# Moving five DMA additions per channel-mixer stage onto VectorE, with a new order of its first pipelined chunk and of some table loads

## The chip, the cores and the metric

One core of one Trainium2 chip runs the whole program in one launch. The metric is the device time of one execution in microseconds. The kernel before takes 1023.12 us in the median of three runs (1019.76 to 1023.62).

## The reference

The function is a decoder trunk of two layers over 256 tokens of width 1024, all in float32. Each layer has three post-norm sublayers:

```
x = LN(a*x + 0.5*swiglu(x, ffn1_w_in, ffn1_w_out))
x = LN(a*x + mixer(x))            # layer 0: differential attention + causal pooling; layer 1: HGRN2
x = LN(a*x + 0.5*swiglu(x, ffn2_w_in, ffn2_w_out))

def swiglu(x, w_in, w_out):       # w_in: 1024 x 5632, w_out: 2816 x 1024
    gate, up = split(x @ w_in, 2)
    return (silu(gate) * up) @ w_out
```

So there are six stages: F0, AB, F1, F2, C, F3. The four F stages are the SwiGLU channel mixers, and the change touches only them.

## The kernel before

**Precision.** Each float32 weight and activation is split into a high part rounded to the matmul type and a low part, the rest. ScalarE makes the high part (`split_hi`, L494 to L500, from `raw` into `w_hi`), VectorE subtracts to get the low part (`split_lo`, L967 to L973, into `w_lo`), and TensorE multiplies high by high, high by low and low by high.

**Weights.** They come in units of 1 MB (128 x 2048 float32) into `raw`, which has three buffers. SyncE issues the loads in order, each in two DMAs, and unit n may start when unit n-3 has been used: for an ordinary unit when its `split_lo` is done (L371 to L380).

**An F stage.** The hidden width 2816 is cut into 11 chunks of 256. Chunks 0, 1 and 10 go the ordinary way. Chunks 2 to 9 (`FIRST_FM` is 2) are pipelined; each takes three units: two of `w_in` (n+1 and n+2 in the code of ScalarE and VectorE, for the *next* chunk) and one of `w_out` (n). In chunks 0 to 9 the down projection of a pair of 128-blocks is not done with eight block products but with seven, of sums of blocks (a Strassen-like scheme): `weight_sums` (L981) and `hidden_sums` (L1011) form the sums on VectorE, `split_sums_hi`/`split_sums_lo` and `hid_early_hi`/`hid_late_hi` and their `_lo` partners split them.

**TensorE in a pipelined chunk** (`feature_chunk`, L2011): `up_block` 0, late products of the chunk before, `up_block` 1, products, `up_block` 2, products, `up_block` 3, products. All four `up_block`s use the one PSUM bank `G[0]`, so each waits (L1978) until ScalarE's `up_copy` (L564 to L570) has copied the block before it out. In a trace `up_block` is the lines L1981 and L1988, a product is L1995.

**Order on ScalarE in a pipelined chunk** (L620 to L636): `split_hi(n+1)`, `hid_early_hi`, `up_copy` 0, `split_hi(n+2)`, `hid_late_hi`, `up_copy` 1, `split_sums_hi`, `up_copy` 2, `split_plain_hi`, `up_copy` 3, `gates_silu`. **On VectorE** (L1176 to L1194): `up_add`, `up_product` and `hidden_sums` of the chunk before, the two parts of `weight_sums`, `hid_early_lo`, `split_lo(n+1)`, `hid_late_lo`, `beside` (table work in some chunks), `split_lo(n+2)`, `split_sums_lo`, `split_plain_lo`.

**GpSimd** adds the two halves of each gate by a DMA with accumulation (`add_gates`, L1694), two per pipelined chunk. In F0 it also loads tables between them: `poolw` (256 KB), `band` (768 KB) and then `ln_gb` (two of 512 KB) follow directly on the gate additions of chunk 3 (L1733 to L1737).

**End of an F stage.** The seven products are combined into the residual `x_tok`. ScalarE copies two of them out (`copied_out`), VectorE forms `kept[1]` and `kept_both` (`sums_out`, L1228, `moved_out`), and GpSimd then adds them to `x_tok` by five accumulating DMAs (`add_sums`, L1703), in an order that its semaphores set. VectorE's `norm_stats` (L1087) waits for these DMAs before it adds the last PSUM sums to `x_tok` and takes the statistics. VectorE's order there (L1196 to L1215) is `sums_out`, `split_lo(n)`, `ffn_hidden`(token tile 0), `split_lo(n+1)`, `last_hidT(0)`, `split_lo(n+2)`, `norm_stats(0)`, half of `norm_gain(0)`, `ffn_hidden`(tile 1), the other half, `last_hidT(1)`, `norm_scale(0)`, `split_lo(n+3)`. TensorE needs `ffn_hidden`(tile 1), line L1137, to transpose the last hidden tile (L1965), and goes on to the next stage behind it.

Of the kernel before, what the change touches and what calls it, by code (L numbers as in the profile page):

```python
# [25 lines left out]
P = 128  # L26
# [49 lines left out]
def build(nc, x, positions, ln_gain, ln_bias, ffn1_w_in, ffn1_w_out, ffn2_w_in, ffn2_w_out, ab_w_in, ab_w_o,  # L76
          diff_lambda, diff_subln, pool_w, pool_scale, c_w_in, c_w_o, c_norm, hgrn_gamma, consts, out):
    with ExitStack() as ctx:
# [3 lines left out]
        def sem(name):  # L82
            return ctx.enter_context(nc.semaphore(name))
# [63 lines left out]
        gate_added = [sem(f"gate_added{j}") for j in range(2)]  # L147
        up_added, x_added = sem("up_added"), [sem(f"x_added{i}") for i in range(5)]
        gate_silu, hid_product = sem("gate_silu"), sem("hid_product")
# [325 lines left out]
        def _(act):  # L475
# [18 lines left out]
            def split_hi(n):  # L494

                if n >= N_UNITS:
                    return
                landed(n)
                freed(free_by[n])
                nc.scalar.copy(w_hi[:, slot_of[n]], raw[:, n % RAW]).then_inc(hi_ready, 1)  # L500
# [77 lines left out]
            def ffn(name, m):  # L578
# [17 lines left out]
                else:  # L596
# [18 lines left out]
                    ffn_silu(name, 1, 1, G[1])  # L615
                split_hi(s0 + 6)
                hidT_copy(name, 1, G[0])
                split_plain_hi(s0 + 7)
                last = NC - 2
                for c in range(FIRST_FM, NC - 1):  # L620
                    n = s0 + 3 * c + 1
                    split_hi(n + 1)
                    hid_early_hi(name, c - 1)
                    up_copy(name, c, 0)
                    split_hi(n + 2)
                    hid_late_hi(name, c - 1)
                    up_copy(name, c, 1)
                    split_sums_hi(name, n)
                    up_copy(name, c, 2)
                    if c == last:  # L630
                        act.wait_ge(plain_used, N_PROD * (f + 1))
                        nc.scalar.activation(kept[0], PROD[0], ACT.Copy, scale=NORMS[name][1]).then_inc(copied_out, 1)
                        split_hi(n + 3)
                    else:
                        split_plain_hi(n + 3)
                    up_copy(name, c, 3)  # L636
                    gates_silu(name, c)
# [320 lines left out]
        def _(dve):  # L958
# [128 lines left out]
            def norm_stats(name, t):  # L1087
                n, factor = NORMS[name]
                y = Y if name in FFN else Y_MIX[name]
                if name in FFN:  # L1090
                    for i in ((2, 4), (0, 1, 3))[t]:
                        dve.wait_ge(x_added[i], 16 * (SILUS[name] + 1))
                for h in range(2):
# [45 lines left out]
            def ffn(name, m):  # L1139
# [38 lines left out]
                for c in range(FIRST_FM, NC - 1):  # L1178
# [10 lines left out]
                    beside(name, c)  # L1189
                    split_lo(n + 2)  # L1190
                    split_sums_lo(name, n)
                    if c < last:
# [11 lines left out]
                ffn_hidden(name, 0, G[0], 4, ffn_tok[:, 1, 0])  # L1204
                split_lo(n + 1)
                last_hidT(name, 0)
                split_lo(n + 2)
                norm_stats(name, 0)
                norm_gain(name, 0, (0,))
# [6 lines left out]
            def beside(name, c):  # L1216
# [8 lines left out]
                if name == BEFORE_C and c in (7, 8, 9):  # L1225
                    lower_bound(c - 7)

            def sums_out(name):  # L1228
# [442 lines left out]
        def _(pool):  # L1671
# [27 lines left out]

            def add_to_x(i, t, cs, part):  # L1700
                pool.dma_start(x_tok[:, t, cs], part, accum_op=ALU.add).then_inc(x_added[i], 16)

            def add_sums(name):  # L1703
                f = SILUS[name]
                low, high = slice(0, 512), slice(512, D)
                pool.wait_ge(copied_out, 2 * f + 1)
                add_to_x(0, 1, high, kept[0])
                pool.wait_ge(copied_out, 2 * f + 2)
                add_to_x(1, 1, low, SUM_PLACES[name][:, 0])
                add_to_x(2, 0, low, SUM_PLACES[name][:, 0])  # L1710
                pool.wait_ge(moved_out, 2 * f + 1)
                pool.wait_ge(x_added[1], 16 * (f + 1))
                add_to_x(3, 1, low, kept[1])
                pool.wait_ge(moved_out, 2 * f + 2)
                pool.wait_ge(x_added[2], 16 * (f + 1))
                pool.dma_start(x_tok[:, 0].rearrange("p (h f) -> p h f", h=2),
                               kept_both.unsqueeze(1).to_broadcast([P, 2, 512]), accum_op=ALU.add
                               ).then_inc(x_added[4], 16)

            pool.wait_ge(lo_ready, RAW + 1)  # L1720
            with nc.allow_non_contiguous_dma(reason="a few columns of parameters"):
# [10 lines left out]
                               ).then_inc(S["pool_tables_landed"], 16)  # L1732
                add_gates("F0", (2, 3))  # L1733
                pool.dma_start(poolw, pool_w[0].rearrange("g p f -> p g f")).then_inc(S["pool_tables_landed"], 16)
                pool.dma_start(band, consts[:, C_BAND:C_DECAY].rearrange("p (g f) -> p g f", g=4)
                               ).then_inc(S["pool_tables_landed"], 16)
            load_gb(0)  # L1737
            for n, name in enumerate(ORDER):
# [18 lines left out]
                if name in FFN:  # L1757
                    add_gates(name, range(4 if name == "F0" else FIRST_FM, NC - 1))
                    add_sums(name)
                norm(n)  # L1760
# [723 lines left out]
```

## Time and profile before

| | |
|---|---|
| median of three runs | 1023.12 us |
| time of the profiled execution | 1022.99 us |
| span of the profile | 1020.4 us |
| TensorE matmul busy | 969.8 us, 95% |
| VectorE busy | 861.3 us, 84% |
| ScalarE busy | 619.4 us, 61% |
| GpSimd busy | 111.1 us, 11% |
| mean granted TensorE clock | 0.975 of full |
| DMA traffic | 199.38 MB, mean 195 GB/s |

The span runs from the first to the last instruction. Granted clock 1.00 is 2.4 GHz and 0.50 is 1.2 GHz. A busy share counts a matmul at the low clock as fully busy, so TensorE's 95% holds slow time too. In timeline rows the bracket gives the idle time of that engine before the row and what ended it.

### The profile page before, as it was taken

What the parts mean: (1) busy time and instruction counts of PE and PEld (TensorE: products, weight loads), DVE (VectorE), ACT (ScalarE), POOL (GpSimd) and SP (SyncE); (2) the same over time, 40 slices, a digit from 0 to 9 for tenths busy, and PEclk for the clock granted to TensorE, in tenths of its full rate; (3) what the DMA queues carried; (4) which work ended last, traced back from release to release, by engine and by line L of the source; (5) the groups of instructions that cost most, each with busy time, mean ns of one, the idle gap of its engine ahead of it and who ended that gap; (6) DMA issues with size and microseconds to landing.
All of it is one profiled execution on the core that took longest, in us unless ns stands there. A gap on an engine that the chain in (4) does not pass through costs nothing.

```text
span 1020.4 us, 13819 instructions
## 1 busy us (share of the span) xinstructions
PE 969.8 (95%) x4904; PEld 818.9 (80%) x4904; DVE 861.3 (84%) x1188; ACT 619.4 (61%) x727; POOL 111.1 (11%) x148
## 2 busy tenths in 40 slices
PE   9798999899998999997989999989999998999995
PEld 7687888688886888885878888868888886888884
DVE  5878998696797899985879999879998997898885
ACT  6566667255745667672656667646898645667660
POOL 0111011100210011011001010200100200011020
PEclk9899999899998999998989999999999998999998
DMA  8767768644557676885476676936432756676862
GB/s 293 242 211 229 240 199 235 195 166 143 191 202 250 188 205 199 246 226 159 163 217 191 211 209 198 282 118 196 133 125 83 241 175 204 184 204 200 245 160 58
DMA packets 141935, 199.38 MB, mean 195 GB/s; under 512 B 7312, under 2 KB 114336, under 8 KB 141744
## 3 DMA queue, kind: packets, MB, share of 16 engines
q1 hardware_dynamic: 126032, 173.56, 52.0%
q0 software_dynamic: 15280, 24.46, 11.6%
q8 instruction: 39, 0.64, 0.3%
q10 hardware_dynamic: 560, 0.52, 0.2%
q14 instruction: 24, 0.20, 0.1%
HBM read 182.78 MB, written 1.05 MB: 180 GB/s over the span
## 4 chain that ended last, share of the span: by engine, by line
PE 72%; DVE 13%; DMA 9%; issue 3%; ACT 2%; POOL 0%; SPq 0%; DVEq 0%; ACTq 0%; POOLq 0%
PE psum L1981 19%; PE psum L1995 12%; PE psum L1988 10%; PE psum L1790 9%; PE psum L1794 9%; PE psum L1799 9%; DMA x_tok<-arena 5%; DVE w_lo L972 4%; DMA raw<-in_ffn_w_in 4%; PE psum L2371 1%; PE psum L1783 1%; DVE w_lo L1008 1%; PE psum L2357 1%; DVE stats L1098 1%; DVE arena L1410 1%
## 5 line engine op out<-in xcount | busy, mean ns | idle before, releaser
L972 DVE TENSOR_TENSOR w_lo<-raw,w_hi 128x2048 fp32r<-128x2048 f32 x125 | 285.1, 2285 | 14.8 <-ACT w_hi L500 14.4
L1981 PE MATMUL psum<-xT,w_hi 128*128 128x512 f32 x1024 | 261.0, 398 | 19.7 <-ACT ffn_tok L570 18.9
L500 ACT CAST w_hi<-raw 128x2048 fp32r<-128x2048 f32 x125 | 237.9, 1911 | 44.8 <-DMA raw<-in_ffn_w_in 32.4
L1981 PEld LDWEIGHTS psum<-xT,w_hi 128*128 128x128 f32 x1024 | 195.7, 192 | 65.8 <-ACT ffn_tok L570 22.8
L1988 PEld LDWEIGHTS psum<-xT,w_lo 128*128 128x128 f32 x1024 | 143.1, 195 | 11.1 <-DVE w_lo L972 0.7
L1988 PE MATMUL psum<-xT,w_lo 128*128 128x256 f32 x1024 | 146.1, 286 | 0.5 <-DVE w_lo L972 0.5
L1790 PE MATMUL psum<-w_hi,xT 128*128 128x512 f32 x447 | 128.6, 398 | 0.5 <-DVE arena L1519 0.4
L1799 PE MATMUL psum<-w_hi,xT 128*128 128x512 f32 x447 | 124.7, 390 | 0.2 <-DVE xT L1076 0.2
L1794 PE MATMUL psum<-w_lo,xT 128*128 128x512 f32 x447 | 124.7, 390 | 0.0
L1698 POOL DMA_DIRECT2D ffn_tok<-ffn_tok x64 | 54.4, 850 | 520.8 <-ACT ffn_tok L570 520.8
L1799 PEld LDWEIGHTS psum<-w_hi,xT 128*128 128x128 f32 x447 | 83.9, 188 | 18.3 <-DVE xT L1076 0.5
L1794 PEld LDWEIGHTS psum<-w_lo,xT 128*128 128x128 f32 x447 | 83.9, 188 | 17.7
L1790 PEld LDWEIGHTS psum<-w_hi,xT 128*128 128x128 f32 x447 | 80.8, 188 | 16.2 <-issue 0.8
L570 ACT COPY arena<-psum 128x512 f32<-128x512 f32 x64 | 37.6, 587 | 92.2 <-PE psum L1988 92.2
L1008 DVE TENSOR_TENSOR w_lo<-arena,w_hi 128x2048 fp32r<-128x2048 f32 x35 | 80.0, 2284 | 10.6 <-ACT w_hi L512 10.6
L978 DVE TENSOR_TENSOR w_lo<-raw,w_hi 128x1536 fp32r<-128x1536 f32 x36 | 63.2, 1755 | 19.3 <-ACT w_hi L506 19.1
L1995 PE MATMUL psum<-w_hi,hT_hi 128*128 128x512 f32 x232 | 76.2, 399 | 0.0
L1995 PE MATMUL psum<-w_lo,hT_hi 128*128 128x512 f32 x232 | 75.4, 395 | 0.3
L512 ACT CAST w_hi<-arena 128x2048 fp32r<-128x2048 f32 x36 | 69.0, 1916 | 3.4 <-DVE arena L996 3.4
L1995 PE MATMUL psum<-w_hi,hT_lo 128*128 128x512 f32 x232 | 69.8, 393 | 0.0
L570 ACT COPY ffn_tok<-psum 128x512 f32<-128x512 f32 x64 | 37.5, 586 | 49.1 <-PE psum L1988 49.1
L506 ACT CAST w_hi<-raw 128x1536 fp32r<-128x1536 f32 x36 | 53.4, 1484 | 11.7 <-PE psum L1995 10.7
(219 smaller groups left out, 1189.5 us busy)
## 6 DMA issues: line engine op xcount, KB each, us to landing
raw<-in_ffn_w_in SPq DMA_DIRECT2D x170, 512.0 KB, 5.4
raw<-in_ffn_w_out SPq DMA_DIRECT2D x88, 512.0 KB, 4.4
raw<-in_c_w_in SPq DMA_DIRECT2D x32, 512.0 KB, 4.7
ffn_tok<-ffn_tok POOLq DMA_DIRECT2D x64, 128.0 KB, 4.5
raw<-in_ab_w_in SPq DMA_DIRECT2D x16, 512.0 KB, 5.4
x_tok<-arena POOLq DMA_DIRECT2D x16, 256.0 KB, 6.3
raw<-in_ab_w_o SPq DMA_DIRECT2D x8, 512.0 KB, 4.4
raw<-in_c_w_o SPq DMA_DIRECT2D x8, 512.0 KB, 4.0
```

Of the source, the lines that this page charges most:

```text
L500: nc.scalar.copy(w_hi[:, slot_of[n]], raw[:, n % RAW]).then_inc(hi_ready, 1)
L512: nc.scalar.copy(w_hi[:, SUMS], SUM_PLACES[name].rearrange("p a f -> p (a f)")).then_inc(sums_hi, 1)
L570: nc.scalar.copy((UPS[name] if b // 2 else GATES)[:, b % 2], G[0]).then_inc(up_copied, 1)
L972: nc.vector.tensor_tensor(w_lo[:, slot_of[n]], raw[:, n % RAW], w_hi[:, slot_of[n]].bitcast(F32), ALU.subtract).then_inc(lo_ready, 1)
L978: nc.vector.tensor_tensor(w_lo[:, PLAIN, 0:1536], raw[:, n % RAW, 512:], w_hi[:, PLAIN, 0:1536].bitcast(F32), ALU.subtract).then_inc(plain ...
L1008: nc.vector.tensor_tensor(w_lo[:, SUMS], SUM_PLACES[name].rearrange("p a f -> p (a f)"), w_hi[:, SUMS].bitcast(F32), ALU.subtract).then_in ...
L1790: nc.tensor.matmul(dst, a_hi, b_hi, start=first, stop=False)
L1794: ins = nc.tensor.matmul(dst, a_hi, b_lo, start=False, stop=final and last)
L1799: ins = nc.tensor.matmul(dst, a_lo, b_hi, start=False, stop=final and last)
L1981: nc.tensor.matmul(G[0], w_hi[:, slot_of[n + kh], at:at + P], xT_both[:, 4 * kh + k].rearrange("p a s -> p (a s)"), start=kh == k == 0, st ...
L1988: ins = nc.tensor.matmul(G[0][:, 0:SEQ], w_lo[:, slot_of[n + kh], at:at + P], xT_hi[:, 4 * kh + k], start=False, stop=kh == 1 and k == 3)
L1995: return nc.tensor.matmul(PROD[p], a[:, A_OF[p] * P:(A_OF[p] + 1) * P], w[:, slot, part * 512:(part + 1) * 512], start=start, stop=stop)
```

## The change

It has four parts. In every F stage the five accumulating DMAs into `x_tok` go, with their semaphores and with the waits in `norm_stats`, and four VectorE additions of 512 columns and one of 1024 take their place: two before `last_hidT(0)` (the 1024-column one adds `kept_both` to both halves of tile 0) and three before `norm_stats(0)`. In the first pipelined chunk (c = 2) of every F stage ScalarE and VectorE take a new order. In F0 alone ScalarE copies the second hidden transposes (`hidT_copy`) before `split_hi(s0+6)`. In F0 GpSimd's table loads are spread: `poolw` behind the gate additions of chunk 4, `band` behind those of chunk 5, `ln_gb` behind those of chunk 6.

```diff
@@ ScalarE, ffn
-                split_hi(s0 + 6)
-                hidT_copy(name, 1, G[0])
+                if m == 0:
+                    hidT_copy(name, 1, G[0])
+                    split_hi(s0 + 6)
+                else:
+                    split_hi(s0 + 6)
+                    hidT_copy(name, 1, G[0])
...
+                    if c == FIRST_FM:
+                        up_copy(name, c, 0)
+                        hid_early_hi(name, c - 1)
+                        split_hi(n + 1)
+                        hid_late_hi(name, c - 1)
+                        up_copy(name, c, 1)
+                        split_sums_hi(name, n)
+                        up_copy(name, c, 2)
+                        split_hi(n + 2)
+                    else:
+                        split_hi(n + 1)
+                        hid_early_hi(name, c - 1)
+                        up_copy(name, c, 0)
+                        split_hi(n + 2)
+                        hid_late_hi(name, c - 1)
+                        up_copy(name, c, 1)
+                        split_sums_hi(name, n)
+                        up_copy(name, c, 2)
@@ VectorE, norm_stats
-                if name in FFN:
-                    for i in ((2, 4), (0, 1, 3))[t]:
-                        dve.wait_ge(x_added[i], 16 * (SILUS[name] + 1))
@@ VectorE, ffn
-                    split_lo(n + 2)
-                    split_sums_lo(name, n)
+                    if c == FIRST_FM:
+                        split_sums_lo(name, n)
+                        split_lo(n + 2)
+                    else:
+                        split_lo(n + 2)
+                        split_sums_lo(name, n)
...
                 split_lo(n + 1)
+                dve.wait_ge(moved_out, 2 * f + 2)
+                add_to_x(0, slice(0, 512), SUM_PLACES[name][:, 0])
+                x0 = x_tok[:, 0].rearrange("p (h f) -> p h f", h=2)
+                step(nc.vector.tensor_tensor(x0, x0, kept_both.unsqueeze(1).to_broadcast([P, 2, 512]), ALU.add))
                 last_hidT(name, 0)
                 split_lo(n + 2)
+                add_to_x(1, slice(512, D), kept[0])
+                add_to_x(1, slice(0, 512), SUM_PLACES[name][:, 0])
+                add_to_x(1, slice(0, 512), kept[1])
                 norm_stats(name, 0)
...
+            def add_to_x(t, cs, part):
+
+                step(nc.vector.tensor_tensor(x_tok[:, t, cs], x_tok[:, t, cs], part, ALU.add))
@@ GpSimd
-            def add_to_x(i, t, cs, part):
-                pool.dma_start(x_tok[:, t, cs], part, accum_op=ALU.add).then_inc(x_added[i], 16)
-
-            def add_sums(name):
...
-                add_gates("F0", (2, 3))
+                add_gates("F0", (2, 3, 4))
                 pool.dma_start(poolw, pool_w[0].rearrange("g p f -> p g f")).then_inc(S["pool_tables_landed"], 16)
+                add_gates("F0", (5,))
                 pool.dma_start(band, consts[:, C_BAND:C_DECAY].rearrange("p (g f) -> p g f", g=4)
                                ).then_inc(S["pool_tables_landed"], 16)
+            add_gates("F0", (6,))
             load_gb(0)
...
-                    add_gates(name, range(4 if name == "F0" else FIRST_FM, NC - 1))
-                    add_sums(name)
+                    add_gates(name, range(7 if name == "F0" else FIRST_FM, NC - 1))
```

## Rows read from the trace of the kernel before

**Rows 1.** Page: the chain's shares, three costly groups, the weight loads' landing time.
```profile
PE 72%; DVE 13%; DMA 9%; issue 3%; ACT 2%; POOL 0%; SPq 0%; DVEq 0%; ACTq 0%; POOLq 0%
...
L972 DVE TENSOR_TENSOR w_lo<-raw,w_hi 128x2048 fp32r<-128x2048 f32 x125 | 285.1, 2285 | 14.8 <-ACT w_hi L500 14.4
...
L500 ACT CAST w_hi<-raw 128x2048 fp32r<-128x2048 f32 x125 | 237.9, 1911 | 44.8 <-DMA raw<-in_ffn_w_in 32.4
...
L978 DVE TENSOR_TENSOR w_lo<-raw,w_hi 128x1536 fp32r<-128x1536 f32 x36 | 63.2, 1755 | 19.3 <-ACT w_hi L506 19.1
...
raw<-in_ffn_w_in SPq DMA_DIRECT2D x170, 512.0 KB, 5.4
```

**Rows 2.** Waits of the whole run: waiter, releaser, us in total, times, longest.
```profile
DVE x_tok L1096 <- DMA x_tok<-arena: 18.9, 3, 8.1
...
PE psum L1981 <- ACT ffn_tok L570: 18.9, 5, 4.2
...
PE psum L1965 <- DVE ffn_tok L1137: 17.4, 3, 7.6
```

**Rows 3.** Timeline of PE, F0 and F1: start us, duration us, instruction.
```profile
39.55 0.62 PE L1995 MATMUL psum<-w_hi,hT_lo 128*128 128x512 f32 x2
...
59.02 1.98 PE L1981 MATMUL psum<-xT,w_hi 128*128 128x512 f32 x8
...
74.95 1.98 PE L1981 MATMUL psum<-xT,w_hi 128*128 128x512 f32 x8
...
316.33 1.98 PE L1981 MATMUL psum<-xT,w_hi 128*128 128x512 f32 x8
...
339.00 1.98 PE L1981 MATMUL psum<-xT,w_hi 128*128 128x512 f32 x8
...
343.15 1.98 PE L1981 MATMUL psum<-xT,w_hi 128*128 128x512 f32 x8
```

**Rows 4.** Timeline of ACT in F1, chunks 2 and 3.
```profile
321.47 1.90 ACT L500 CAST w_hi<-raw 128x2048 fp32r<-128x2048 f32 x1 [4.70 <-DMA raw<-in_ffn_w_in]
...
323.90 0.58 ACT L570 COPY ffn_tok<-psum 128x512 f32<-128x512 f32 x1
...
341.97 0.59 ACT L570 COPY ffn_tok<-psum 128x512 f32<-128x512 f32 x1
```

**Rows 5.** Timeline of DVE in F1, chunk 2: first weight sum, then chunk 3's first step.
```profile
320.48 1.22 DVE L990 TENSOR_TENSOR arena<-raw 128x1024 f32<-128x1024 f32 x1
...
338.66 0.69 DVE L1044 TENSOR_TENSOR arena<-arena 128x512 f32<-128x512 f32 x1 [0.29 <-ACT arena L570]
```

**Rows 6.** Windows: stretch, PE, PEld, DVE, ACT, POOL busy, granted clock, DMA share, GB/s.
```profile
83.20:86.00 2.80, 0.00 (x0) 0.00 (x0) 0.49 (x2) 2.73 (x4) 0.00 (x0) 1.00 0.91 303
324.50:331.10 6.60, 6.57 (x21) 5.59 (x22) 5.18 (x4) 3.26 (x4) 1.04 (x2) 0.57 0.91 274
198.20:203.80 5.60, 5.60 (x15) 4.32 (x16) 4.53 (x5) 0.38 (x1) 0.00 (x0) 0.50 0.00 0
477.60:481.90 4.30, 4.27 (x14) 3.47 (x15) 3.70 (x5) 0.37 (x1) 0.00 (x0) 0.68 0.00 0
671.90:676.30 4.40, 4.36 (x14) 3.56 (x15) 3.81 (x5) 0.37 (x1) 0.00 (x0) 0.66 0.01 4
533.50:550.20 16.70, 16.70 (x90) 14.42 (x89) 16.36 (x18) 11.54 (x13) 1.68 (x2) 1.00 0.65 184
```

**Rows 7.** Chain of F0's chunk 3: start us, us, what.
```profile
70.34 12.91 DMA raw<-in_ffn_w_in
```

**Rows 8.** Timeline of DVE at the end of F1.
```profile
462.24 0.42 DVE L1242 TENSOR_TENSOR hT_lo<-psum,hT_hi 128x256 fp32r<-128x256 f32 x1 [1.67 <-ACT hT_hi L653]
...
473.00 0.69 DVE L1096 SCALAR_TENSOR_TENSOR x_tok<-psum,x_tok 128x512 f32<-128x512 f32 x1 [8.14 <-DMA x_tok<-arena]
```

**Rows 9.** Timeline of PE at the end of F3, which had no such wait.
```profile
1005.50 0.38 PE L1965 MATMUL psum<-ident,ffn_tok 128*128 128x128 f32 x2
...
1008.45 0.62 PE L1790 MATMUL psum<-w_hi,hT_hi 128*128 128x512 f32 x2
```

More of the change, by code:

```diff
@@ L147, in build @@
         gate_added = [sem(f"gate_added{j}") for j in range(2)]
-        up_added, x_added = sem("up_added"), [sem(f"x_added{i}") for i in range(5)]
+        up_added = sem("up_added")
         gate_silu, hid_product = sem("gate_silu"), sem("hid_product")
@@ L621, in ffn @@
                     n = s0 + 3 * c + 1
[L622 to L629, printed above, removed]
+                    if c == FIRST_FM:
[16 more added lines that the diff above has]
+                        up_copy(name, c, 2)
                     if c == last:
@@ L1698, in add_gates @@
                         pool.dma_start(GATES[:, j, 0:SEQ], GATES[:, j, SEQ:], accum_op=ALU.add).then_inc(gate_added[j], 16)
-            def add_to_x(i, t, cs, part):
-                pool.dma_start(x_tok[:, t, cs], part, accum_op=ALU.add).then_inc(x_added[i], 16)
-            def add_sums(name):
[L1704 to L1718, printed above, removed]
             pool.wait_ge(lo_ready, RAW + 1)
```

## The prediction

> **What bounds the kernel now.** I read the chain of waits first. TensorE is 72% of the way to the end, and what is not TensorE is mostly VectorE and DMA [rows 1]. So the question is where TensorE stands still, and the list of waits answers it. Two waits stand out: five times it waits for ScalarE's `up_copy` before an `up_block`, 18.9 us in all, and three times for VectorE's `ffn_hidden` before it transposes the last hidden tile, 17.4 us in all [rows 2]. The timelines put the first kind at chunk 2 of all four F stages and once in chunk 4 of F0, the second at the ends of F0, F1 and F2. The windows add a second loss: behind the long stalls the granted clock is low, 0.57 for 6.6 us in F1's chunk 2, 0.50 (1.2 GHz), 0.68 and 0.66 at the three ends, while behind the 2.80 us stall of F0's chunk 4 it never left 1.00 [rows 6]. VectorE's 84% busy share is no bound there: VectorE is itself waiting in those places.
>
> **Part 1, the additions to x.** In F1 VectorE stands 8.14 us before `norm_stats(0)`, for the accumulating DMAs [rows 8]; over the three stages it is 18.9 us, and three times, so F3 has none of it [rows 2]. The change removes the wait and adds five operations. An addition of 512 columns with both operands in SBUF takes 0.69 us, one of 1024 columns 1.22 us [rows 5], and each waits for its own signal, some 0.04 us. Before `last_hidT(0)` come 0.73 + 1.26 = 2.0 us, where VectorE had 1.67 us idle [rows 8]; 0.3 us sticks out. Before `norm_stats(0)` come 3 x 0.73 = 2.2 us. So each stage pays 2.5 us from its wait and the gain is 18.9 - 3 x 2.5 = 11.4 us. It reaches the end in full, because `ffn_hidden`(tile 1) follows `norm_stats(0)` at a fixed distance and TensorE stands for it: its 17.4 us become 6.0, 2.0 in each stage. In F3 the five operations fall into gaps in front of TensorE's last sums and cost 0; if that cover were gone they would cost 2.2 us. GpSimd loses five DMA issues a stage and nothing is queued behind them but the `rstd` power, which waits for VectorE anyway. What is late next is VectorE's own string from `norm_stats(0)` to `ffn_hidden`.
>
> **Part 2, the clock at these ends.** From the transposes to the next stage's transposes TensorE took 5.6, 4.3 and 4.4 us at clocks 0.50, 0.68 and 0.66 [rows 6]. The same instructions took 1008.45 - 1005.50 = 2.95 us in F3, after no such stall [rows 9]. With a stall of 2.0 us, below the 2.80 us that left the clock at 1.00 [rows 6], I expect 2.4 GHz to be kept: gain 2.65 + 1.35 + 1.45 = 5.4 us. Bounds are 0 and 5.4; I take 5.4, since 2.0 lies under the nearest row. The Trainium skill (TensorE: Matmul & The Clock Gate, Part 4, on transposes) speaks against this: a transpose does not count as engine activity in the way a matmul does, so the two transposes behind the stall would lengthen the quiet stretch. No row here separates that. By it the sum would be 5.4 us smaller, which is the first rival below.
>
> **Part 3, the first pipelined chunk.** A steady chunk takes 74.95 - 59.02 = 15.93 us. F1's chunk 2 takes 339.00 - 316.33 = 22.67, a surplus of 6.7 [rows 3]. Its cause is ScalarE's order: `up_copy` 0 sits behind `split_hi(n+1)`, which stands 4.70 us for its weights, so that the copy starts at 323.90 [rows 4], though the block, begun at 316.33, needs only some 3 us. F2 and F3 repeat the pattern with surpluses of 6.7 and 7.0. In F0 a front part waits for other things: from the end of its late products (39.55 + 0.46) to 59.02 it takes 19.0, where a steady chunk has 15.93 - (343.15 - 339.00) = 11.8, surplus 7.2 [rows 3]. All of it includes the low clock, so all is removable: 27.6 us. In the new order the copy goes first and waits for TensorE alone. The load of n+1 lands at the same moment as before, its cast runs beside `up_block` 1, and `up_copy` 1 is ready some 0.6 us before it is needed.
>
> Something is given back. `split_hi(n+2)` now sits behind `up_copy` 2, which can run only when the third block is done. The second block starts 4.15 after the chunk, the third 11.8 / 3 = 3.9 later, and it runs 3 us: in F1's times 316.33 + 4.15 + 3.9 + 3 = 327.4. Then follow the copy 0.5, the cast 1.9, `split_lo(n+2)` 2.2 and `split_plain_lo` 1.7 [rows 1] (`split_sums_lo`, moved ahead, fills VectorE's wait for that cast and costs nothing; uncovered it would cost another 2.2): VectorE reaches chunk 3's first step at 333.7 instead of 338.66 [rows 5], a gain of 5.0, while TensorE would start chunk 3 at 339.00 - 6.7 = 332.3. VectorE thus is at +1.4 beside TensorE, where it was at -0.3. The chain through `hidden_sums`, `hid_early_hi` and `up_copy` 0 has 343.15 - (341.97 + 0.59) = 0.6 us of slack [rows 3, 4]. So TensorE stands 1.4 + 0.3 - 0.6 = 1.1 us once in chunk 3, too short for the clock, and VectorE catches up in the rest of that chunk. Gain 5.6 in F1 and 5.9 in F0 and F3. In F2 VectorE is the bound behind chunk 2 (16.36 of 16.70 us busy, a chunk in 16.7 instead of 15.93 us) [rows 6], so only its own gain of 4.9 counts. Sum 5.9 + 5.6 + 4.9 + 5.9 = 22.3 us. F0's early `hidT_copy` I cost at nothing: its block then ends its high passes sooner but still waits for `split_lo(s0+6)`, which does not move. If that cover were gone it would give up to 0.7.
>
> **Part 4, the tables.** In F0 the second load of chunk 3 lands after 12.91 us [rows 7], against 5.4 in the median [rows 1]; 2 MB of tables (`poolw`, `band`, `ln_gb`) were issued just ahead. TensorE stands 2.80 us for it [rows 6]. Spread over three chunks the largest piece is 1 MB: at (12.91 - 5.4) / 2 = 3.8 us per MB it delays one load by 3.8, and the load had room for 12.91 - 5.4 - 2.8 = 4.7. Gain 2.8; bounds 0 and 2.8. GpSimd's gate additions that the tables are moved past come first, so nothing of chunk 4 or 5 waits for them, and the tables are read a hundred microseconds later.
>
> **Sum.** 11.4 + 5.4 + 22.3 + 2.8 = 41.9 us off the profiled execution's 1022.99 gives 981.1; this execution stands 0.13 under the median of 1023.12, so 981.
>
> **Rivals.**
> *The clock stays low at the ends of F0, F1 and F2.* For it: TensorE still stands 2.0 us, with transposes behind. Against: 2.80 us did nothing. Part 2 falls away: 986.5. Chance 0.13.
> *Weights late in chunk 3.* In chunk 2 the DMA engines are already 0.91 busy at 274 GB/s [rows 6], and the load that follows `split_lo(n+2)` is issued only as TensorE enters chunk 3, so it lands when ScalarE wants it, without slack. At 3 us late in each of four stages 12 us go back: 993. Against: the load before it has landed by then, and 5.4 us just does. Chance 0.17.
> *The lag does not fade, and the kernel gets slower.* Loads wait for `split_lo` three units back, so a late subtraction makes a late load, a late cast and a late subtraction again. Place: chunks 3 to 9 of each F stage and the last one, 32 chunks in all. If each kept a stall like the 2.8 us of F0's chunk 4, 90 us would be lost against 42 gained: 1071. It decides from 42 / 32 = 1.3 us per chunk. Against: VectorE idles some 1.2 us in a plain chunk, so a lag shrinks. Chance 0.04.
> *The change does not do what it says.* If the additions cannot start where they stand, because TensorE or GpSimd still holds one of their operands, or the copies move without effect, the time stays within 5 us of before: 1020. The DMAs that read the same operands were on their way before VectorE's idle time began, so chance 0.02.
> *VectorE does not lag in chunk 3*, so that the 1.1 us in three stages and F2's share come back too: 977. Chance 0.12.
>
> **How the numbers follow.** My forecast of 981 has 0.52. The range must reach the clock rival and the late weights and the case without the lag: 974 to 997, which leaves out the last cases of slow and no effect and a margin. About 0.5%, or 5 us, is what a measurement of this kernel can tell from no change. Faster by more than that: 0.52 + 0.13 + 0.17 + 0.12 = 0.94. Within it: the change without effect, 0.02. Slower: 0.04.
>
> **What would show it.** In the changed profile VectorE's wait for x DMAs is gone; `norm_stats(0)` of F1 starts about 5.6 us sooner relative to its stage's last products; TensorE's three stalls there are 2.0 us and the windows behind show clock 1.00 and 2.95 us. In chunk 2 TensorE runs through at clock 1.00; in chunk 3 it stands about 1.1 us before `up_block` 1; F2 gains less than the rest. In F0 no load takes over 10 us. I would be wrong on part 3 if chunk 3 or later chunks exceed 15.93 by more than 1.2 us in F1, on part 2 if the clock after a 2 us stall is below 1.00, on part 1 if the additions take more than 0.75 us each.

## The result, and the profile after

The changed kernel takes 982.13 us in the median of four runs (980.97 to 982.53). Its ratio to the kernel before, run beside it, is 0.9603 with a 95% interval of [0.958, 0.9626]. The forecast was 981 in a range of 974 to 997. The profiled execution took 982.20 us with a span of 980.5 us. TensorE's mean granted clock rose from 0.975 to 0.997, and DMA traffic fell from 199.38 to 193.10 MB. One run of the kernel before, beside the second group of experiments below, took 1198.9 us at a granted clock of 0.748 and is left out of the ratios.

The page of the kernel after: busy time of TensorE and VectorE, the chain's shares, and two of the groups that [rows 1] shows of before.

```profile
PE 955.4 (97%) x4904; PEld 805.7 (82%) x4904; DVE 875.5 (89%) x1208; ACT 619.6 (63%) x727; POOL 93.5 (10%) x128
...
PE 77%; DVE 15%; ACT 3%; DMA 2%; issue 2%; SPq 1%; POOL 0%; DVEq 0%; ACTq 0%
...
L986 DVE TENSOR_TENSOR w_lo<-raw,w_hi 128x2048 fp32r<-128x2048 f32 x125 | 285.2, 2285 | 20.3 <-ACT w_hi L500 19.7
...
L500 ACT CAST w_hi<-raw 128x2048 fp32r<-128x2048 f32 x125 | 238.2, 1913 | 26.2 <-DMA raw<-in_ffn_w_in 15.4
```

TensorE's share of the chain went from 72 to 77% and DMA's from 9 to 2%. The two groups take the same time for each instruction as before; only their idle time differs. So nothing became faster in itself: 969.8 us of TensorE busy time became 955.4 because less of it ran at the low clock, and the rest of the gain is idle time that went.

The waits of the whole run, after (waiter, releaser, us in total, times, longest), to lay beside [rows 2]:

```profile
ACT w_hi L500 <- DMA raw<-in_ffn_w_in: 15.4, 16, 2.4
...
PE psum L1972 <- DVE ffn_tok L1148: 5.4, 3, 1.8
...
PE psum L1988 <- ACT ffn_tok L570: 4.4, 6, 1.0
```

VectorE's wait of 18.9 us for the additions to `x_tok` has no row any more. TensorE's wait for `up_copy` went from 18.9 to 4.4 us and that for `ffn_hidden` from 17.4 to 5.4.

TensorE at the ends of F0, F1 and F2 after (start us, duration us, instruction, idle before): the transposes of the last hidden tile, and those of x for the next stage.

```profile
186.63 0.44 PE L1972 MATMUL psum<-ident,ffn_tok 128*128 128x128 f32 x2 [1.80 <-DVE ffn_tok L1148]
...
189.67 1.04 PE L1790 MATMUL psum<-ident,x_tok 128*128 128x128 f32 x8
...
452.50 0.44 PE L1972 MATMUL psum<-ident,ffn_tok 128*128 128x128 f32 x2 [1.82 <-DVE ffn_tok L1148]
...
638.43 0.44 PE L1972 MATMUL psum<-ident,ffn_tok 128*128 128x128 f32 x2 [1.81 <-DVE ffn_tok L1148]
```

The window behind the first of these stalls (PE, PEld, DVE, ACT, POOL busy, granted clock, DMA share, GB/s), beside the 0.50 of [rows 6]:

```profile
186.60:189.60 3.00, 2.97 (x14) 2.49 (x15) 2.66 (x5) 0.37 (x1) 0.00 (x0) 1.00 0.00 0
```

Each stall is 1.8 us, the clock behind it 1.00, and the way to the next transposes 3.04 us where it was 5.6.

VectorE at the end of F0 after, which holds all five additions:

```profile
175.34 0.68 DVE L1252 TENSOR_TENSOR x_tok<-x_tok,arena 128x512 f32<-128x512 f32 x1
176.06 1.22 DVE L1224 TENSOR_TENSOR x_tok<-x_tok,arena 128x1024 f32<-128x1024 f32 x1
...
179.86 2.14 DVE L1252 TENSOR_TENSOR x_tok<-x_tok,arena 128x512 f32<-128x512 f32 x3
182.03 0.69 DVE L1107 SCALAR_TENSOR_TENSOR x_tok<-psum,x_tok 128x512 f32<-128x512 f32 x1
```

The three additions of tile 1 take 182.03 - 179.86 = 2.2 us directly ahead of tile 0's statistics, and 2.2 is more than the 1.8 for which TensorE still stands.

What they replaced can be read more closely than the prediction did. The chain of waits of the kernel before at the end of F1:

```profile
451.62 7.59 DMA x_tok<-arena
...
461.04 11.88 DMA x_tok<-arena
```

The last of the five DMAs (`kept_both` onto tile 0) was issued at 461.04, behind GpSimd's wait of 6.40 us for one of the earlier ones to land, and landed 11.88 us later at 472.92; the statistics started at 473.00 [rows 8]. The other four had landed by 465.40. So it was one DMA, late in its place and long in itself, that held VectorE there. Whether the same five DMAs in another order, tile 0's first, would have removed part of the wait was not tried.

TensorE in chunks 2 and 3 of F1 after (`up_block` 0 and 2 of chunk 2, 0 and 1 of chunk 3, and the start of chunk 4), beside [rows 3]:

```profile
301.94 1.98 PE L1988 MATMUL psum<-xT,w_hi 128*128 128x512 f32 x8
...
310.43 2.11 PE L1988 MATMUL psum<-xT,w_hi 128*128 128x512 f32 x8 [0.25 <-ACT ffn_tok L570]
...
318.42 1.98 PE L1988 MATMUL psum<-xT,w_hi 128*128 128x512 f32 x8
323.70 2.12 PE L1988 MATMUL psum<-xT,w_hi 128*128 128x512 f32 x8 [0.97 <-ACT ffn_tok L570]
...
335.62 1.98 PE L1988 MATMUL psum<-xT,w_hi 128*128 128x512 f32 x8
```

Chunk 2 takes 16.48 us instead of 22.67, chunk 3 17.20 instead of 15.93.

### The profile page after: what moved, and what is told of

Same layout as the page of the kernel before. It is cut to its first block, busy times and chain, and to the rows that moved or that the text cites. A ratio compares the mean times of both kernels' runs of the same rounds, so it can differ in the third digit from the quotient of the medians.

```text
span 980.5 us, 13807 instructions
## 1 busy us (share of the span) xinstructions
PE 955.4 (97%) x4904; PEld 805.7 (82%) x4904; DVE 875.5 (89%) x1208; ACT 619.6 (63%) x727; POOL 93.5 (10%) x128
## 2 busy tenths in 40 slices
DMA packets 138544, 193.10 MB, mean 197 GB/s; under 512 B 6992, under 2 KB 114016, under 8 KB 138352
## 4 chain that ended last, share of the span: by engine, by line
PE 77%; DVE 15%; ACT 3%; DMA 2%; issue 2%; SPq 1%; POOL 0%; DVEq 0%; ACTq 0%
PE psum L1988 19%; PE psum L2002 12%; PE psum L1797 10%; PE psum L1801 10%; PE psum L1806 10%; PE psum L1995 10%; DVE w_lo L986 5%; DMA raw<-in_ffn_w_in 2%; ACT w_hi L500 2%; PE psum L2378 1%; PE psum L1790 1%; DVE w_lo L1022 1%; DVE x_tok L1252 1%; PE psum L2364 1%; DVE arena L1436 1%
## 5 line engine op out<-in xcount | busy, mean ns | idle before, releaser
L1988 PE MATMUL psum<-xT,w_hi 128*128 128x512 f32 x1024 | 254.9, 391 | 4.7 <-ACT ffn_tok L570 4.4
L1988 PEld LDWEIGHTS psum<-xT,w_hi 128*128 128x128 f32 x1024 | 191.1, 188 | 50.8 <-ACT ffn_tok L570 10.1
L1995 PEld LDWEIGHTS psum<-xT,w_lo 128*128 128x128 f32 x1024 | 139.7, 190 | 11.6 <-DVE w_lo L986 1.6
L1995 PE MATMUL psum<-xT,w_lo 128*128 128x256 f32 x1024 | 143.0, 282 | 1.4 <-DVE w_lo L986 1.4
```

Source lines behind the costliest of these rows:

```text
L1988: nc.tensor.matmul(G[0], w_hi[:, slot_of[n + kh], at:at + P], xT_both[:, 4 * kh + k].rearrange("p a s -> p (a s)"), start=kh == k == 0, st ...
L1995: ins = nc.tensor.matmul(G[0][:, 0:SEQ], w_lo[:, slot_of[n + kh], at:at + P], xT_hi[:, 4 * kh + k], start=False, stop=kh == 1 and k == 3)
```

## The experiments

Twelve kernels ran, in three groups of four, each group beside runs of the kernel before. The medians of before beside them were 1021.86, 1021.82 (without the run of 1198.9 us) and 1021.52 us, against 1023.37 beside the kernel after; ratios are therefore safer than differences between groups of less than some 2 us.

**The additions alone.** Into the kernel before go only the five VectorE additions, and its accumulating DMAs and waits go out.

```diff
+                dve.wait_ge(moved_out, 2 * f + 2)
+                add_to_x(0, slice(0, 512), SUM_PLACES[name][:, 0])
...
                 norm_stats(name, 0)
...
-                    add_sums(name)
```

> The kernel before with the five additions of each F stage on VectorE and nothing else of the change. My theory (parts 1 and 2): TensorE's three stalls at the ends of F0, F1, F2 (5.05, 7.64, 4.67 us) shrink to about 2 us each (-11.4) and the granted clock behind them stays at 1.00 (-5.4): 1023 - 16.8 = 1006 us. Rival, the clock falls even behind a 2 us stall: 1012. Rival, the additions only pay beside the new chunk order: over 1015.

Measured: 1004.02 us (1001.27 to 1007.71), ratio 0.9826 [0.9791, 0.9862], 17.8 us off where 16.8 were expected. Two windows of this run, behind the stalls of 1.81 and 1.82 us at the ends of F0 and F1 (columns as in the window above):

```profile
194.70:197.70 3.00, 2.97 (x14) 2.49 (x15) 2.65 (x5) 0.37 (x1) 0.00 (x0) 1.00 0.00 0
465.50:468.50 3.00, 3.00 (x11) 2.48 (x12) 2.65 (x5) 0.37 (x1) 0.00 (x0) 0.74 0.01 3
```

The size is confirmed within the interval, which reaches from 14 to 21 us, and the additions need no help from the new order. In the profiled execution (1004.07 us, 18.9 off) 15.8 us of the gain lie at the three ends; 2.7 more lie in chunks 2 and 3, where the stalls are about as long as before and the low clock behind them was shorter. But the same stall in front of the same instructions left the clock at 1.00 in F0 and F2 and lowered it in F1. My bound ("2.0 lies under the nearest row") is thereby no bound.

**The order alone.** The kernel before with the new chunk 2 on both engines:

```diff
+                    if c == FIRST_FM:
+                        up_copy(name, c, 0)
+                        hid_early_hi(name, c - 1)
+                        split_hi(n + 1)
...
+                        split_sums_lo(name, n)
+                        split_lo(n + 2)
```

> The kernel before with the new order of chunk 2 on ScalarE and VectorE and nothing else. My theory (part 3): 5.6 + 5.9 + 4.9 + 5.9 = 22.3 us off, 1001 us; read off the trace of the kernel after, some 20 us, 1003. A 1 us stall before the second block of chunk 3 in each F stage, and the 2.8 us stall of F0's chunk 4 still there or larger, as its tables are not moved. Rival, late weights when only the order is changed: over 1008.

Measured: 1003.95 us (1000.45 to 1010.31), ratio 0.9816 [0.9783, 0.9849], 17.9 us off. Each chunk 3 has the expected stall (0.93 to 0.98 us). What is missing to 22.3 us lies at least in part in F0's chunk 4. Its load in the chain of waits, and TensorE behind it:

```profile
62.84 13.88 DMA raw<-in_ffn_w_in
```

```profile
79.81 3.78 PE L1995 MATMUL psum<-xT,w_hi 128*128 128x512 f32 x8 [6.01 <-ACT ffn_tok L570]
```

```profile
79.80:86.40 6.60, 6.59 (x21) 5.60 (x22) 6.11 (x9) 3.13 (x4) 1.05 (x2) 0.55 0.58 159
```

The stall of 2.80 us [rows 6] is now 6.01, with the clock at 0.55 for 6.6 us behind it: 3.2 us of stall and 3.0 of clock, which the order loses in this execution, with the tables together. Parts 3 and 4 are not additive. This profiled execution, at 1010.31 us, is the slowest of the six: in it chunks 2 and 3 give 21.2 us, chunk 4 takes 5.9 and the three ends, where the DMAs still add to `x_tok`, take 3.1 more than in the profile of before. How much chunk 4 takes in the other five is not shown.

**The tables alone.**

```diff
-                add_gates("F0", (2, 3))
+                add_gates("F0", (2, 3, 4))
                 pool.dma_start(poolw, ...)
+                add_gates("F0", (5,))
                 pool.dma_start(band, ...)
...
+            add_gates("F0", (6,))
```

> The kernel before with the table loads of F0 spread over chunks 4 to 6 and nothing else. My theory (part 4): the 2.8 us stall in F0's chunk 4 goes and nothing comes in its place: 1020.3 us, ratio 0.997. Rival, the load is late for another reason, as unit loads queue behind each other: no change, 1023.

Measured: 1018.63 us in 12 runs (1015.93 to 1020.41), ratio 0.9958 [0.9935, 0.9981]: 3.2 us off, and no stall of TensorE in F0's chunk 4.

**The tables together again, in the kernel after.**

```diff
-                add_gates("F0", (2, 3, 4))
+                add_gates("F0", (2, 3))
                 pool.dma_start(poolw, ...)
-                add_gates("F0", (5,))
...
-            add_gates("F0", (6,))
```

> The kernel after with the F0 table loads in their old places, all 2 MB behind the gate additions of chunk 3. By my part 4 as predicted the 2.8 us stall of chunk 4 comes back and nothing more: 985. What the run with the order alone showed speaks against it: there the same stall had grown to 6.0 us with a slow block behind it. Theory now: with the new order the next loads are wanted sooner, nothing covers more of the tables' time, and the price is that stall of 6 us and some 1.7 us of clock: 982.1 + 7.7 = 990.

Measured: 987.88 us (987.06 to 989.97), ratio 0.9657 [0.9627, 0.9688], 5.8 us more than after. The load in the chain, ScalarE's cast that waits for it, and TensorE:

```profile
62.77 12.39 DMA raw<-in_ffn_w_in
```

```profile
75.19 1.90 ACT L500 CAST w_hi<-raw 128x2048 fp32r<-128x2048 f32 x1 [5.61 <-DMA raw<-in_ffn_w_in]
```

```profile
78.25 3.52 PE L1986 MATMUL psum<-xT,w_hi 128*128 128x512 f32 x8 [4.52 <-ACT ffn_tok L570]
```

The stall is 4.5 us, between the two expectations, and it costs clock as well (this execution, at 989.97 us, is the slowest of the four). The same edit is worth 3.2 us in the kernel before and 5.8 in this one; the intervals of the two overlap, so it is the rows that tell them apart. It is not the same load that is late. ScalarE's two casts of chunk 4 in the kernel before:

```profile
75.01 1.90 ACT L500 CAST w_hi<-raw 128x2048 fp32r<-128x2048 f32 x1
...
83.27 1.90 ACT L500 CAST w_hi<-raw 128x2048 fp32r<-128x2048 f32 x1 [4.77 <-DMA raw<-in_ffn_w_in]
```

There the first `w_in` unit (its halves issued at 67.25 and 67.83, the second landing after 6.01 us) came in time, and the second unit, issued at 69.78 and 70.34 behind all four tables (67.56 to 69.38), was the late one; its cast stands behind `up_copy` 0 and stops TensorE before the third block. With the new order and the tables together it is the first unit, whose second half is issued at 62.77 between the first table (62.02) and the other three (62.79 to 63.85) and takes 12.39 us. Its cast stands ahead of `up_copy` 0, so TensorE stops one block sooner and for longer; the second cast then waits for nothing. Why this half takes 12.39 us where the same half took 6.01 is not settled by these rows.

**Tile 1's additions as DMAs, tile 0's on VectorE.**

```diff
                 split_lo(n + 2)
-                add_to_x(1, slice(512, D), kept[0])
-                add_to_x(1, slice(0, 512), SUM_PLACES[name][:, 0])
-                add_to_x(1, slice(0, 512), kept[1])
                 norm_stats(name, 0)
...
+                if name in FFN and t == 1:
+                    for i in range(3):
+                        dve.wait_ge(x_added[i], 16 * (SILUS[name] + 1))
...
```

In the part left out GpSimd issues three accumulating DMAs again, each on its own semaphore.

> The kernel after, but the three additions to token tile 1 are accumulating DMAs again, issued by GpSimd as before and waited for only ahead of the statistics of tile 1; the two additions to tile 0 stay on VectorE. My theory: the remaining 1.8 us stall at each end is VectorE's string, of which 2.2 us are these three additions, and the DMAs have some 17 us until tile 1's statistics; statistics of tile 0 start when its last sums are done, and TensorE gains 1.8 us in each of F0, F1, F2: 982.1 - 5.4 = 976.7 us, unless VectorE then holds up the next stage's tile 1, which leaves at least 1 us a stage: 979. Rival, the DMAs are late for tile 1 or their traffic delays a weight load: no gain or a loss, 982 or more.

Measured: 975.31 us (974.88 to 975.72), ratio 0.954 [0.9511, 0.9569], below the expectation of 976.7 and clear of the interval of the kernel after. VectorE and TensorE at the end of F0:

```profile
179.55 0.68 DVE L1110 SCALAR_TENSOR_TENSOR x_tok<-psum,x_tok 128x512 f32<-128x512 f32 x1
...
183.71 0.42 DVE L1151 TENSOR_TENSOR ffn_tok<-psum,ffn_tok 128x256 f32<-128x256 f32 x1
```

```profile
184.39 0.38 PE L1984 MATMUL psum<-ident,ffn_tok 128*128 128x128 f32 x2
```

The statistics start where the three additions had stood, the hidden product is ready at 184.1, and TensorE transposes without a stall. VectorE has no wait for an x DMA in this run. So the remaining 1.8 us of the kernel after were its own additions, and three DMAs are fast enough for tile 1's statistics.

**up_copy 0 first in chunk 3 as well**, on top of that kernel.

```diff
                     else:
                         split_hi(n + 1)
-                        hid_early_hi(name, c - 1)
-                        up_copy(name, c, 0)
+                        if c == FIRST_FM + 1:
+                            up_copy(name, c, 0)
+                            hid_early_hi(name, c - 1)
+                        else:
+                            hid_early_hi(name, c - 1)
+                            up_copy(name, c, 0)
```

> The kernel with tile 1's additions as DMAs (975.3 us) and, in chunk 3 of each F stage alone, up_copy 0 ahead of hid_early_hi on ScalarE. Theory of part 3's give-back: the stall before the second block of chunk 3 comes because up_copy 0 stands behind hid_early_hi, which waits for VectorE's late hidden_sums; with the copy first the stalls (0.6 to 1.0 us in each of four stages) go: 975.3 - 3.2 = 972 us. Rival, VectorE's lag then stops TensorE one step later, at the products that need the hidden split: no gain.

Measured: 972.14 us (970.92 to 973.97), ratio 0.9512 [0.9481, 0.9543], the fastest kernel of the study and the 3.2 us below the run before it that were expected. The two ratios' intervals overlap, but the ranges (970.92 to 973.97, 974.88 to 975.72) do not, and in the rows the four stalls are gone. The chain's shares on its page, and TensorE's one remaining stall of over 0.5 us in any chunk 3, in F2:

```profile
PE 87%; DVE 8%; ACT 1%; issue 1%; DMA 1%; POOL 0%; DVEq 0%; SPq 0%; ACTq 0%
```

```profile
510.90 0.73 PE L2018 MATMUL psum<-w_lo,hT_hi 128*128 128x512 f32 x2 [0.89 <-DVE w_lo L1026]
```

The give-back of part 3 was the place of `up_copy` 0 behind a step that needs `hidden_sums`. VectorE starts chunk 3 of F1 1.41 us behind TensorE, as late as in the kernel after; the copy simply does not need it. Only in F2, where VectorE has table work too, does its lateness reach TensorE elsewhere.

**VectorE's order in chunk 2 undone.**

```diff
-                    if c == FIRST_FM:
-                        split_sums_lo(name, n)
-                        split_lo(n + 2)
-                    else:
-                        split_lo(n + 2)
-                        split_sums_lo(name, n)
+                    split_lo(n + 2)
+                    split_sums_lo(name, n)
```

> The kernel after with VectorE's split_lo(n+2) ahead of split_sums_lo again in chunk 2, ScalarE's order unchanged. By part 3 of the prediction the swap fills VectorE's wait for the cast, and without it split_sums_lo is 2.2 us on the way to chunk 3's first step and to TensorE's products of the sums: 982.1 + up to 4 x 2.2 = 986 to 991 us. Rival, the slack takes it: 982.

Measured: 994.24 us (991.91 to 996.52), ratio 0.9735 [0.969, 0.9781], 12.1 us more than after. VectorE and TensorE in F1's chunk 2:

```profile
319.05 2.29 DVE L986 TENSOR_TENSOR w_lo<-raw,w_hi 128x2048 fp32r<-128x2048 f32 x1 [3.41 <-ACT w_hi L500]
321.26 2.28 DVE L1022 TENSOR_TENSOR w_lo<-arena,w_hi 128x2048 fp32r<-128x2048 f32 x1
```

```profile
323.60 0.72 PE L1998 MATMUL psum<-w_lo,hT_hi 128*128 128x512 f32 x2 [2.86 <-DVE w_lo L1022]
```

TensorE stands 2.86 us in all four stages, and then no more in chunk 3; behind two of the four stalls the clock fell. I had bounded the swap by its 2.2 us. It is worth more, some 3 us a stage: ScalarE's new order makes VectorE stand 3.41 us for the cast, and without the swap the low part of the sums, which TensorE wants in this very chunk, stands behind that wait.

**F0's hidT_copy undone.**

```diff
-                if m == 0:
-                    hidT_copy(name, 1, G[0])
-                    split_hi(s0 + 6)
...
+                split_hi(s0 + 6)
+                hidT_copy(name, 1, G[0])
```

> The kernel after with F0's second hidT_copy behind split_hi(s0+6) again. Prediction: nothing, 982.1; the wait for the copy (0.72 us) comes back and the wait for the low part of s0+6 shrinks by as much (1.37 to 0.5). Rival, the early copy delays the split by its own length and costs 0.2 us: 981.9. Both are within what a run can tell, so the rows decide: the start of chunk 2 relative to the split's end.

Measured: 981.69 us (980.69 to 983.71), ratio 0.9612 [0.9569, 0.9654]: nothing, as forecast. The start of F0's chunk 2 in this run, and the same wait in the kernel after:

```profile
34.66 2.11 PE L1984 MATMUL psum<-xT,w_hi 128*128 128x512 f32 x8 [0.73 <-ACT arena L547]
...
37.71 0.74 PE L1991 MATMUL psum<-xT,w_lo 128*128 128x256 f32 x4 [0.47 <-DVE w_lo L982]
```

```profile
38.28 0.74 PE L1995 MATMUL psum<-xT,w_lo 128*128 128x256 f32 x4 [1.37 <-DVE w_lo L986]
```

0.73 + 0.47 = 1.20 us in two waits became 1.37 in one. The cover named in the prediction, `split_lo(s0+6)`, is what holds.

**Longer stalls at the ends.** Three kernels add one, two and five additions on dead scratch to the kernel after, in F0 to F2:

```diff
+                if name != "F3":
+                    for _ in range(2):
+                        step(nc.vector.tensor_tensor(kept[1], kept[1], kept[0], ALU.add))
                 norm_stats(name, 0)
```

With two:

> The kernel after with two further additions of 512 columns (on dead scratch) ahead of the statistics of tile 0 in F0, F1 and F2, 1.45 us each stage, to lengthen TensorE's stall at each end from 1.8 to 3.3 us, with the transposes behind it as before. Theory: the clock stays at 1.00 (in F0's chunk 4 it did behind 2.8 us), and the time rises by 3 x 1.45 = 4.4 us to 986.5. Rival, with transposes behind a stall the clock falls sooner: 1.3 to 2.7 us more for each end, 991 to 994.

With five:

> As the run with two further additions, but with five, 3.6 us each stage: stalls of 5.4 us, as long as before the change. Theory: the low clock comes back too, as it was behind 4.7 to 7.6 us: 982.1 + 3 x 3.6 + 3 x 1.8 = 998 us, and the windows behind the stalls show 0.5 to 0.7. Rival, the low clock before was not of the stall but of what else ran there (the DMAs): 993, clock 1.00.

With one:

> The kernel after with one further addition ahead of the statistics of tile 0 in F0, F1 and F2: stalls of 2.5 us with transposes behind, between 1.8 us (the clock stayed at 1.00 in three of three in the kernel after, and fell in one of three with the additions alone) and 3.25 us (it fell in three of three). If the clock stays: 982.1 + 2.2 = 984.3 us. If it falls each time: 989. I expect it to fall in some and not in others, with a scatter between the runs: 986.

Measured: two 992.09 us (990.44 to 993.76), ratio 0.9698 [0.9663, 0.9732]; five 998.84 (997.82 to 1000.06), ratio 0.9771 [0.974, 0.9802]; one 987.26 (986.89 to 988.46), ratio 0.9662 [0.962, 0.9703]. TensorE's stalls at F0 and F2 with one addition:

```profile
187.91 0.44 PE L1975 MATMUL psum<-ident,ffn_tok 128*128 128x128 f32 x2 [2.52 <-DVE ffn_tok L1148]
...
643.90 0.44 PE L1975 MATMUL psum<-ident,ffn_tok 128*128 128x128 f32 x2 [2.55 <-DVE ffn_tok L1148]
```

From there to the next transposes of x (192.40, 646.93) it is 4.49 us in F0 and 3.03 in F2: the clock fell in the first, and in F1, and stayed in F2; 982.1 + 2.2 + 2 x 1.5 = 987.3. With two additions it fell in all three, and with five too (0.59 for 4.7 us in F0). A window behind the stall at F0's end, with two additions:

```profile
188.00:192.50 4.50, 4.48 (x14) 3.68 (x15) 3.90 (x5) 0.37 (x1) 0.00 (x0) 0.63 0.00 0
```

The sums close: two additions 982.1 + 4.4 of stall + (4.58 + 4.61 + 5.60 - 3 x 3.04) of clock = 992.2; five 982.1 + 10.9 + (4.80 + 4.40 + 4.77 - 3 x 3.04) = 997.8. So my theory for 3.3 us was wrong and its rival's time came (whether because of the transposes, as the rival has it, these runs cannot tell), and the theory for 5.4 us was right. A fall costs 1.4 to 2.6 us here and no more behind 5.4 us than behind 3.3.

**Stalls in the middle of a stage**, with no transposes behind, on the kernel with tile 1's additions as DMAs:

```diff
+                for _ in range({("F0", 5): 4, ..., ("F3", 8): 6}.get((name, c), 0) if b == 0 else 0):
+                    step(nc.scalar.copy(GATES[:, 0], G[0]))
                 nc.scalar.copy((UPS[name] if b // 2 else GATES)[:, b % 2], G[0]).then_inc(up_copied, 1)
```

> The kernel with tile 1's additions as DMAs (975.3 us), with up_copy 0 repeated on ScalarE 4 to 8 times in chunks 5 and 8 of the F stages, so that TensorE stands in the middle of a stage, with matmuls and no transposes behind: 4 times (about 1.9 us of stall) in F0's chunk 5 and F2's chunk 8, 5 (2.6) in F1's 5 and F0's 8, 6 (3.2) in F2's 5, F1's 8 and F3's 8, 8 (4.5) in F3's 5. Theory: the clock depends on how long TensorE stood and not on the transposes: it stays at 1.00 behind 1.9 and falls behind 3.2 and more, as at the ends (three of three at 3.25). Rival, transposes count as rest: without them the clock stays at 1.00 behind 3.2 us too. Stalls alone give 975.3 + 22 = 997 us; each fall adds 1.5 to 2, so 1003 by the theory, 998 to 1000 by the rival.

Measured: 1003.96 us (1002.86 to 1005.83), ratio 0.9825 [0.9781, 0.9869]. Five of the eight stalls (timeline of TensorE):

```profile
91.73 3.44 PE L2002 MATMUL psum<-xT,w_hi 128*128 128x512 f32 x8 [1.86 <-ACT ffn_tok L572]
...
144.15 2.11 PE L2002 MATMUL psum<-xT,w_hi 128*128 128x512 f32 x8 [2.38 <-ACT ffn_tok L572]
...
413.36 3.50 PE L2002 MATMUL psum<-xT,w_hi 128*128 128x512 f32 x8 [3.00 <-ACT ffn_tok L572]
...
604.69 2.12 PE L2002 MATMUL psum<-xT,w_hi 128*128 128x512 f32 x8 [1.76 <-ACT ffn_tok L572]
...
940.33 2.12 PE L2002 MATMUL psum<-xT,w_hi 128*128 128x512 f32 x8 [3.00 <-ACT ffn_tok L572]
```

Windows behind three of them (PE busy, granted clock, DMA share, GB/s):

```profile
91.70:97.70 6.00, 5.97 (x23) 0.72 1.01 306
...
413.30:419.30 6.00, 5.95 (x24) 0.74 0.99 309
...
940.30:946.30 6.00, 5.97 (x30) 1.00 1.01 300
```

The first group's duration tells the clock at a glance: 3.4 to 3.5 us at the low one, 2.1 at the full. It fell behind 1.86 us and not behind 1.76 or 2.38 (twice); of two stalls of 3.00 us in the same place of the chunk it fell behind one; it fell behind 3.75 and 4.24. The theory's order by length holds only at the long end, and the rival as put (no fall behind 3 us) falls too. The time that the theory gave, 1003, came out all the same: the eight stalls add up to 22.4 us, which leaves 6.3 for the four falls.

## Why the prediction was right

The time and the case were right: 982.1 against 981, and none of the rivals came. By its terms, from the two profiled executions (1022.99 to 982.20 us, 40.8 off):

| term | forecast, us | in the traces | by a run of its own |
|---|---|---|---|
| 1 and 2, additions and clock at three ends | 16.8 | 17.1 | 17.8 |
| 3, order of chunk 2 | 22.3 | 20.2 | 17.9 alone |
| 4, tables | 2.8 | 3.0 | 3.2 alone, 5.8 in the kernel after |
| elsewhere | 0 | 0.5 | |

Of the 40.8 us, 0.9 lie outside the profile's span, which became shorter by 39.9.

**Part 1** stands as worked out. The stall at each end is 1.80 to 1.82 us where 2.0 were forecast: a stage pays 2.3 us and not 2.5 for its additions. 17.4 - 5.4 = 12.0 against 11.4. Each addition costs 0.69 + 0.04 as read, and TensorE lost nothing in F3: between its two last hidden transposes it takes 8.41 us, as before 8.43.

**Part 2** had the right number for a reason that failed. The ways behind the stalls are 3.04, 3.04 and 3.05 us where 2.95 were forecast, a gain of 5.2 for 5.4. But the step "I take 5.4, since 2.0 lies under the nearest row" took one row at 2.80 us for a safe side. The tally over all profiled executions of this study (before, after and the twelve, a stall counting as fallen when the clock went below 1.00 in the 6 us behind it) is:

| TensorE stood, us | transposes behind: fell | matmuls behind: fell |
|---|---|---|
| 1.7 to 1.9 | 1 of 15 | 1 of 2 |
| 2.3 to 2.9 | 2 of 3 | 2 of 8 |
| 3.0 to 3.3 | 3 of 3 | 1 of 2 |
| 3.7 and more | 12 of 12 | 16 of 16 |

So at 1.8 us the clock nearly always stays, at 2.8 us it is a toss-up that the row of before happened to win, and a stall of the length that I forecast had no wall in front of it, only good odds. The chance of 0.13 for the low clock at all three ends was, by one fall in 15, rather high than low; no stall between 1.9 and 2.3 us was run. One more thing in that step was not what it seemed: the row cited for "the 2.80 us that left the clock at 1.00" covers the stall itself and not what follows it, and in several runs the clock fell only once TensorE had resumed. The window behind bears the reading out:

```profile
86.00:92.00 6.00, 5.99 (x30) 5.12 (x31) 5.83 (x8) 3.84 (x3) 0.86 (x1) 1.00 0.68 191
```

By the prediction's own sign ("if the clock after a 2 us stall is below 1.00") part 2 held in the kernel after and failed in F1 of the kernel with the additions alone.

Whether transposes matter is not settled. Between 2.3 and 3.3 us the clock fell in 5 of 6 cases with them and in 3 of 10 without. That leans the way of the Trainium skill (TensorE: Matmul & The Clock Gate, Part 4), by which a transpose doesn't count as activity as a matmul does; but 14 of 15 stalls of 1.8 us with transposes behind left the clock alone, so the rule took nothing away here, and the cases are too few to give it a price.

**Part 3** had its mechanism right and its size 2.1 us too high. (By its own surplus of 7.2 us F0 should have been put down at 6.1 and not 5.9, which would have made it 2.3.) By stage the gains are 5.6, 4.9, 4.25 and 5.5 us for 5.9, 5.6, 4.9 and 5.9. The lag of VectorE in F1's chunk 3 was forecast at 1.4 us and is 319.84 - 318.42 = 1.42:

```profile
319.84 0.69 DVE L1058 TENSOR_TENSOR arena<-arena 128x512 f32<-128x512 f32 x1
```

Two terms were mis-sized. First, "`up_copy` 1 is ready some 0.6 us before it is needed": it is 0.25 us late. ScalarE in that chunk:

```profile
304.90 0.59 ACT L570 COPY ffn_tok<-psum 128x512 f32<-128x512 f32 x1 [2.53 <-PE psum L1995]
...
307.68 1.92 ACT L500 CAST w_hi<-raw 128x2048 fp32r<-128x2048 f32 x1 [1.56 <-DMA raw<-in_ffn_w_in]
...
309.80 0.58 ACT L570 COPY ffn_tok<-psum 128x512 f32<-128x512 f32 x1
```

The load's landing still sets the second copy; the change only took the first out from behind it. Second, the stall in chunk 3 comes in all four stages (0.93 to 0.97 us for 1.1 in three), in F2 on top of its bound by VectorE, and the chunk is 1.27 us longer for it (17.20 - 15.93), as the block behind a stall takes 2.12 instead of 1.98. In F1: 22.67 - 16.48 - 1.27 = 4.92. The prediction had said that it would be wrong on part 3 if the chunk exceeded 15.93 by more than 1.2 us; by that sign it is, by a hair, in size and not in mechanism. From chunk 4 on a chunk takes 15.93 us again, so the lag fades as argued and the slower case had no footing; no load was late in chunk 3 either.

The swap of `split_sums_lo` was called free and was; its bound of 2.2 us, should the cover go, was too low: undone it costs 12.1 us over four stages.

**Part 4** is right at 3.0, and in the kernel after no load of F0 takes over 9.5 us, but the sum treated it as independent of part 3, and it is not. Without it part 3 would have met a stall of 4.5 to 6 us in place of 2.8, for another load than the one that the prediction looked at. The room of 4.7 us that it gave the load held in the order of before only.

## What to carry to other kernels

When a DMA that feeds an engine is replaced by work on that engine, ask of each addition who needs it first: here only one of five landed too late for its reader, and moving tile 1's three as well cost 1.8 us of TensorE at each of three ends, 6.4 us in all by the two ratios (0.9603 - 0.954, of 1022 us). A copy that frees a bank for TensorE belongs ahead of anything on its engine that waits for a load or for another engine, and the reordering shifts the wait to the next such place (chunk 2 to chunk 3), which is worth a second look with the same eye. Price two parts of a change together where both act on one queue: the tables' spreading was worth 3.2 us in one order and 5.8 in the other by the medians, and 3.1 and 6.2 us of chunk 4 in the profiled executions.

## What was not expected of the hardware

The granted clock is not a function of the length of a stall. The same stall of 3.00 us, at the same place of chunk 8 with the same instructions and nearly the same DMA traffic behind it (309 and 300 GB/s), was followed by 0.74 in one stage and 1.00 in another, and 1.82 us at the end of F1 gave 0.74 in one kernel and 1.00 in another. The first microseconds cut from a long stall were worth more than their length: 17.8 us of time (14 at the least, by the interval) for the 12.0 of stall that the additions removed. For the 5.4 that were left it was 6.4, where the difference of 1.0 is within the noise.

Whether the scatter between runs comes from the clock is not shown. The kernel before took between 1017.35 and 1029.14 us in 17 runs on one chip, at mean granted clocks of 0.981 and 0.971 in the fastest and the slowest, and the kernel with tile 1's additions as DMAs, whose longest stall past the program's start is 1.4 us, took 974.88 to 975.72. But the fastest kernel, with no longer stall either, took 970.92 to 973.97, and the one with three stalls of 2.5 us only 986.89 to 988.46.
